# Columns of x on SyncE's queue, a pair's last quarter ahead of the down sums, gate results at the key latents' place

## The reference

```python
z = u @ w_in[l]                      # u = rms_norm(h, g_mix[l])
c_q, c_kv, k_r, rq, rk, rv, rg, gates = jnp.split(z, cuts, axis=-1)
q = (rms_norm(c_q, g_q_lat[l]) @ w_uq[l]).reshape(B, S, MLA_HEADS, MLA_NOPE + MLA_ROPE)
kv = (rms_norm(c_kv, g_kv_lat[l]) @ w_ukv[l]).reshape(B, S, MLA_HEADS, MLA_NOPE + MLA_V)
o_a = causal_block_attention(q_full, k_full, v_a, ...)
y_a = o_a.reshape(B, S, MLA_WIDTH) @ w_proj_mla[l]
y_r = (jax.nn.silu(rg) * y_ret) @ w_proj_ret[l]
g_a, g_r = jnp.split(jax.nn.sigmoid(gates + b_gate[l]), 2, axis=-1)
h = h + (g_a * y_a + g_r * y_r) @ w_out[l]
```

## Time and profile before

| | |
|---|---|
| median of 3 runs | 1813.04 us (1811.16 to 1816.38) |
| the profiled execution | 1813.21 us |
| its span, first to last instruction | 1811.4 us |
| TensorE busy | 1745.7 us, 96% |
| VectorE busy | 1175.9 us, 65% |
| GpSimd busy | 958.8 us, 53% |
| ScalarE busy | 734.4 us, 41% |
| mean granted TensorE clock | 0.991 |

### The profile page before, as it was taken

One profiled execution on the slowest core, in us unless ns is written; L12 is line 12 of the kernel. 1 busy time (PEld: TensorE's weight loads), 2 busy tenths in 40 slices (PEclk: granted clock), 3 DMA queues, 4 the chain that ended last, 5 costly groups with the idle time before them and its releaser, 6 DMA issues. The chain is left out here.

```text
span 1811.4 us, 25039 instructions
## 1 busy us (share of the span) xinstructions
PE 1745.7 (96%) x8527; PEld 1454.3 (80%) x8527; DVE 1175.9 (65%) x1637; ACT 734.4 (41%) x1307; POOL 958.8 (53%) x564
## 2 busy tenths in 40 slices
PE   7999999999989899979999999999999999999998
PEld 7888888888777777768878888778888888878887
DVE  5655663555757777864245554878777777889842
ACT  7422223333315666611133331644454444444432
POOL 6743333335564777634432322487777777665540
PEclk9999999999999999999999999999999999999999
DMA  6611111326763888481221224243333433494322
GB/s 267 208 47 35 41 40 47 117 88 219 272 227 137 324 315 305 172 279 70 93 81 47 70 82 162 71 133 118 124 134 106 139 122 109 163 334 160 122 76 93
DMA packets 119634, 260.30 MB, mean 144 GB/s; under 512 B 7936, under 2 KB 58752, under 8 KB 115072
## 3 DMA queue, kind: packets, MB, share of 16 engines
q1 hardware_dynamic: 84656, 180.03, 29.7%
q10 hardware_dynamic: 34896, 79.18, 11.9%
HBM read 184.73 MB, written 73.92 MB: 143 GB/s over the span
## 5 line engine op out<-in xcount | busy, mean ns | idle before, releaser
L724 POOL TENSOR_SCALAR wh<-raw 128x1024 fp32r<-128x1024 f32 x59 | 167.7, 2842 | 414.0 <-PE ps L841 380.4
L1636 ACT ACTIVATE wh<-raw 128x512 fp32r<-128x512 f32 (+1 forms) x200 | 128.0, 651 | 133.7 <-PE ps L1517 58.1
L773 POOL TENSOR_TENSOR wl<-raw,wh 128x512 fp32r<-128x512 f32 x88 | 136.7, 1564 | 72.1 <-ACT wh L1636 70.9
L841 PE MATMUL ps<-uh,wh 128*128 128x512 f32 x368 | 147.3, 400 | 6.4 <-DVE cql L2491 5.7
L760 POOL TENSOR_TENSOR over_rings<-over_rings 128x512 f32<-128x512 f32 x92 | 118.2, 1286 | 52.8 <-DMA over_rings<-in_slabs 47.3
L726 POOL TENSOR_TENSOR wl<-raw,wh 128x1024 fp32r<-128x1024 f32 x59 | 143.1, 2425 | 4.9
L847 PE MATMUL ps<-uh,wl 128*128 128x512 f32 x368 | 144.7, 393 | 0.0
L846 PE MATMUL ps<-ul,wh 128*128 128x512 f32 x368 | 144.5, 393 | 0.0
L816 POOL TENSOR_TENSOR wl<-raw,wh 128x512 fp32r<-128x512 f32 x63 | 94.4, 1507 | 74.2 <-ACT wh L1636 74.1
L2491 DVE SCALAR_TENSOR_TENSOR ya<-zA,sm,ya 128x512 f32<-128x512 f32 x88 | 109.6, 1245 | 31.9 <-ACT ya L2315 24.8
L1587 PE MATMUL ps<-mvh_,wh 128*128 128x512 f32 x252 | 98.3, 390 | 1.2 <-DVE mvl_ L2488 1.0
(11 more groups left out here) (529 smaller groups left out, 5292.8 us busy)
## 6 DMA issues: line engine op xcount, KB each, us to landing
raw<-in_slabs SPq DMA_DIRECT2D x106, 512.0 KB, 3.6
over_rings<-in_slabs SPq DMA_DIRECT2D x22, 1024.0 KB, 7.1
s_s<-over_rings SPq DMA_DIRECT2D x22, 1024.0 KB, 4.9
ssm<-s_s SPq DMA_DIRECT2D x22, 512.0 KB, 4.5
raw<-s_s SPq DMA_DIRECT2D x22, 512.0 KB, 3.7
s_f<-yb ACTq DMA_DIRECT2D x22, 512.0 KB, 5.3
raw<-s_d SPq DMA_DIRECT2D x36, 256.0 KB, 2.5
raw<-in_slabs SPq DMA_DIRECT2D x27, 256.0 KB, 4.8
```

What stands on the lines that cost most here:

```text
L724: pool.tensor_scalar(wh[:, j, :], raw[:, j % RAWS, :], 1.0, None, ALU.mult).then_inc(S["w_hi"], 1)
L773: pool.tensor_tensor(wl[:, v // 2, half(v % 2)], src, wh[:, v // 2, half(v % 2)].bitcast(f32), ALU.subtract).then_inc(S["v_ready"], 1)
L841: l = pe.matmul(o, lh, rh, start=start, stop=False, skip_group_check=onto)
L1636: return act.activation(o, i, ACT.Copy, **kw)
```

## The change

It has three parts.

1. The columns of x are issued by SyncE. `vr` is laid out head by head, so that head m has the 4 KB of column m, and a column's load waits for `m_pv` of its head. Columns 0 and 1 are issued in the ring's loop (n = 13 and 17), 2 to 4 behind the second mix slab, 5 behind the fourth, 6 and 7 behind the third and the fourth slab of w_out.
2. In the gate pairs, VectorE makes c21 of a pair at the end of that pair's round and ahead of A1 and the down sums, and no longer at the start of the next round. In the last round c21 and the product B0 come ahead of the down sums.
3. gzA and gzB move to the place of ckh and ckl, and gu2, gu4, gx1, gyB1, gyA and gyB0 to that of cqh and cql. The wait for the last gate stores moves on ScalarE from ahead of the first latents to ahead of ckh, behind the first query rows. VectorE waits for its own last product (`gp_mul`) in place of the stores.

```diff
+COLUMN_AT = (13, 17)
+COLUMN_BEHIND = {1: (2, 3, 4), 3: (5,), 6: (6,), 7: (7,)}
...
-        gu2, gu4, gzA, gzB, gyA, gyB1, gyB0, gx1, dsum_gates = place(64, [
-            ("gu2", [P, H2], 0), ("gu4", [P, H2], 0), ("gzA", [P, T], 0), ("gzB", [P, T], 0), ("gyA", [P, T], 0),
-            ("gyB1", [P, H2], 0), ("gyB0", [P, 2, H2], 0), ("gx1", [P, H2], 0), ("dsum_gates", [P, 2, T], 0)])
+        gu2, gu4, gx1, gyB1, gyA, gyB0, gzA, gzB, dsum_gates = place(64, [
+            ("gu2", [P, H2], 0), ("gu4", [P, H2], 0), ("gx1", [P, H2], 0), ("gyB1", [P, H2], 0), ("gyA", [P, T], 0),
+            ("gyB0", [P, 2, H2], 0), ("gzA", [P, T], 0), ("gzB", [P, T], 0), ("dsum_gates", [P, 2, T], 0)])
...
-        vr, qrow, qr1, qr2 = place(0, [("vr", [P, NT, MH, 2, DV], 1),
+        vr, qrow, qr1, qr2 = place(0, [("vr", [P, MH, NT, 2, DV], 1),
...
+            def residual_in(m):
+
+                sp.wait_ge(S["m_pv"], 2 * m + 2)
+                sp.dma_start(hT[:, m, :].rearrange("p (t n) -> p t n", t=NT),
+                             x[:, m * P:(m + 1) * P].rearrange("(t p) n -> p t n", p=P)).then_inc(
+                    S["x_ld0" if m < CH else "xc_ld"], 16)
+
+            def mix_slab(s):
+                sp.wait_ge(S["w_ready"], s - RAWS + 1)
+                sp.dma_start(raw[:, s % RAWS, :], slabs[s - 2 * KB]).then_inc(S[f"ld{s % RAWS}"], 16)
...
+                if n in COLUMN_AT:
+                    residual_in(COLUMN_AT.index(n))
...
-            slab_loads(SLAB0["mix"], SLAB0["xo"], 2 * KB)
+            for s in range(SLAB0["mix"], SLAB0["out"] + SLOTS):
+                mix_slab(s)
+                for m in COLUMN_BEHIND.get(s - SLAB0["mix"], ()):
+                    residual_in(m)
+            slab_loads(SLAB0["out"] + SLOTS, SLAB0["xo"], 2 * KB)
...
-            for name in ("zA0", "zA1", "zB0", "zB1"):
-                act.wait_ge(*gz_store(name, GP))
             for j in range(4):
...
                 if t == 0:
+                    for name in ("zA0", "zA1", "zB0", "zB1"):
+                        act.wait_ge(*gz_store(name, GP))
                     for b in range(2):
                         act.wait_ge(S["l_c"], b + 1)
                         copy(ckh[:, half(b)], lz[:, QB, half(b)]).then_inc(S["l_hi"], 1)
...
-            for m in range(CH):
-                residual_in(m)
-
-
             for m in range(KB):
...
-                if m < CH:
-                    residual_in(CH + m)
...
-                if i:
-                    quarter(i - 1, "c21")
                 quarter(i, "u2")
...
                 quarter(i, "c12")
+                if more:
+                    quarter(i, "c21")
                 if i >= 2:
                     gate_times(i, "A1")
+                if not more:
+                    quarter(i, "c21")
+                    gate_times(i, "B0")
                 if i >= 1:
                     down_sums(i - 1)
-            quarter(GP - 1, "c21")
-            gate_times(GP - 1, "B0")
-
-
-            for name in ("zA0", "zA1", "zB0", "zB1"):
-                dve.wait_ge(*gz_store(name, GP))
+
+
+            dve.wait_ge(S["gp_mul"], gm_at(GP - 1, "B0"))
```

More of the change, by code:

```diff
@@ L1280, in m_pv @@
                     qs = slice(max(0, c - CH * b) * P, H2)
-                    l = pe.matmul(ps[:, 1, qs], vr[:, c, h, :, :].rearrange("p a n -> p (a n)"), p[:, c, qs],
+                    l = pe.matmul(ps[:, 1, qs], vr[:, h, c, :, :].rearrange("p a n -> p (a n)"), p[:, c, qs],
                                   start=k == 0, stop=k == len(each) - 1, skip_group_check=True)
@@ L2007, in value_rows_hi @@
                 act.wait_ge(S["v_done"], MB + t + 1)
-                copy(vr[:, t, :, 0, :], ps[:, 2 + t % 4, :].rearrange("p (h n) -> p h n", h=MH)).then_inc(S["v_evh"], 1)
+                copy(vr[:, :, t, 0, :], ps[:, 2 + t % 4, :].rearrange("p (h n) -> p h n", h=MH)).then_inc(S["v_evh"], 1)
             for t in range(NT):
@@ L2917, in value_rows_lo @@
                 dve.wait_ge(S["v_evh"], t + 1)
-                lo(vr[:, t, :, 1, :], ps[:, 2 + t % 4, :].rearrange("p (h n) -> p h n", h=MH),
-                   vr[:, t, :, 0, :]).then_inc(S["v_lo"], 1)
+                lo(vr[:, :, t, 1, :], ps[:, 2 + t % 4, :].rearrange("p (h n) -> p h n", h=MH),
+                   vr[:, :, t, 0, :]).then_inc(S["v_lo"], 1)
             R = slice(NOPE, QK)
```

## The result

| | before | changed |
|---|---|---|
| median, runs taken side by side | 1812.57 us (4 runs) | 1793.24 us (1791.27 to 1796.82, 4 runs) |
| ratio, 95% interval | | 0.9892 [0.9870, 0.9914] |
| profiled execution: span | 1811.4 us | 1795.0 us |
| mean granted clock of it | 0.991 | 0.991 |

The kernel is faster by 19.3 us; forecast were 22.8.

What follows compares the result with a forecast made beforehand. TensorE's queue was taken to bound the kernel; 12.3 (mix) + 1.6 (gu) + 8.9 (latents) = 22.8 us off the profiled 1813.2 gave 1790.4 us, range 1787.0 to 1798.8.

Steps and rivals of the forecast that it cites:

- Mix wait: TensorE before the output product: 10.1 us idle plus half clock behind it, held by ScalarE's column issues; gain 12.3 us.
- Waits on gu: TensorE's two waits on ScalarE's copy of a gate pair's first product go with c21 sooner; gain 1.6 us.
- Latent wait: TensorE's wait on cql, low half of the query latents: 5.9 us plus 3.0 of half clock, gain 8.9 us.
- Last pair: Last gate pair before the latents: cql written near 508.5, at 512.8 if two products are stretched; no stall taken.
- Rival 1: Down sums between B0 and cql are stretched and make the latents late: 1795.2 us, chance 0.15.
- Columns in the ring: Columns 0 and 1 in SyncE's up-sums ring before the mix slabs: 3 us each against 8.2 cover, costing nothing.
- rivals 3 and 4: Ring ends late: 3, 6.4 us a column, 1798.0 us (0.08); 4, issue and landing stop it, 1829.4 us (0.02).
- Rival 2: Mix hangs on tiles in a full DMA system, only four issues' time is won: 1798.5 us, chance 0.08.
- Attention: Stretch from the query rows' first product to the first product on oth: forecast gain 0.
- The rest: Stretch from the first product on ach to the end, code not touched: forecast gain 0.

Runs made afterwards that it cites:

- columns_alone: Kernel before with part 1 alone (columns of x issued by SyncE, vr head by head): 1801.25 us, ratio 0.9942.
- two_on_scalar: Changed kernel with columns 2 and 3 of x issued by ScalarE again, ahead of its first mih: 1800.62 us, ratio 0.9925.
- order_alone: Kernel before with part 2 alone (VectorE's new order) and vr head by head, waits on the gate stores kept: 1806.13 us, ratio 0.9968.
- order_columns: Changed kernel with part 3 undone (gate tiles and waits on their last stores as before): 1792.02 us, ratio 0.9873.
- sums_first: Changed kernel with the last round's order as before, four down sums ahead of c21 and B0: 1794.49 us, ratio 0.9887.
- columns_late: Changed kernel with all columns issued by SyncE during the mix, behind the sixth, seventh and eighth mix slabs: 1796.17 us, ratio 0.9893.

## Why the prediction was right, and where it was off

- **Mix wait, 12.3 us: right.** 11.7 to 12.3 us in the three profiles (mix and the stretch behind it). columns_alone has it alone, two_on_scalar brings it back. Wrong was a picture beside it: VectorE was to catch up early and then follow TensorE. It had work until the end and cost 0.4 us, because its products are stretched by GpSimd's splits (mil 2.90 us in place of 0.69) about once in 11 us, which I had counted only around the latents. From the first mil to the last a half-block took it 2.38 us, not the 1.93 of the prediction.
- **Waits on gu, 1.6 us: right.** Both are gone.
- **Latent wait, 8.9 us: the total about right, its ground wrong.** I booked it to the moved waits. The profile of order_alone shows that the new order alone removes it, and order_columns that the new places add nothing that can be measured. The step that failed was to take the store's wait as fixed: its landing moves with the last product, and I had computed that the product comes some 9 us sooner. The size was off as well: with gu the step earned 9.4, 7.8 and 10.2 us of the 10.5. In two of the three profiles a new stretch at half clock behind the 32 light products took 1.7 and 3.4 us back; and before's own wait varies (5.7 and 3.1 us in the two profiles that have it).
- **Last pair, no stall: right, with less room than it sounds.** Forecast was cql between 508.5 and 512.8, measured 511.02. The longest stretch fell on a sum (2.86 us). Rival 1 was 1.2 us away. Where its order was undone (sums_first) a wait of 1.6 us stood.
- **Columns in the ring, 3 us each under a cover of 8.2: too dear.** With two, four or none the ring ended alike within its spread of 2 us. The first mix slab was split by 739.84 and first used at 748.01, again 8.2 us ahead, 1.2 of which is the longer wait on prow. Nothing of what rivals 3 and 4 forecast came.
- **Rival 2, only the issuing is saved:** its 5.9 us of wait did not come; of its mechanism columns_late shows 1.1 us. Its rule is that another issuing engine saves only the sequencer's time, usually small beside the DMA's (the Trainium skill, DMA: Bandwidth & Descriptors, section "Issuing engines are not separate DMA queues"). The first half held here. The second did not: two issues held ScalarE for 9.3 us in two_on_scalar, in front of work.
- **Attention, nothing: 0.4 to 1.4 us lost.** The step that failed was to let the attention move as one block. GpSimd's first split falls elsewhere against VectorE's otl. In the nine profiles whose third otl took 2.0 us or more the attention took 199.8 to 200.9 us, in the five others 198.7 to 199.5. Why the split moved is in part open: with no column in the ring wl began 0.9 to 2.1 us ahead of that otl, with columns 0.1 to 0.6 in eight of nine profiles (2.1 in sums_first), so the columns may have a share in it. The Trainium skill, SBUF — State Buffer, section "Who interferes with whom", says that of two such instructions the second waits for the first; here the otl that began within wl ended 0.54 to 0.56 us behind wl's end in all 14 profiles. Beside wh, the other half of the split, the rule holds only in part (last section). I had used the rule for the latents and not for this place.
- **The rest, nothing:** 3.3, -0.2 and 2.2 us against one profile of before. Code that no kernel touched took 889.4 to 895.1 us, and its time at half clock accounts for these differences to 1.2 us. That the change has no part in it is not shown: the three profiles without part 1 have 3.4 to 6.8 us at half clock there, the eleven with it 3.4 to 13.7.

## What to carry to other kernels

A wait for a DMA is gone as soon as the DMA is issued early enough: when a change moves both the issue and the wait, price each alone, or one of them may be superfluous. A DMA issue can hold its engine for microseconds: one of these columns took 0.96 us in the ring and 4.7 us on average behind twelve gate tiles. So such loads belong on an engine with nothing urgent behind them, and early. No run here shows whether the number of pieces or the tiles ahead make them dear. When all work in front of a stage moves, look again at every pair of VectorE and GpSimd instructions near a wait: their overlap changes, and 2 us more for one of them cost TensorE 1.2 us here.

## What the runs showed that I had not expected

- Which of GpSimd's instructions holds VectorE: above all the one of the split that has two inputs (wl<-raw,wh). Every VectorE instruction of 128x512 with two inputs in SBUF that began within a 128x1024 wl ended 0.54 to 0.56 us behind it, 294 of 294 in the 14 profiles (starts within 0.02 us of wl's left out): otl, the sum at 507.08 (wl there until 509.39), the product at 502.88 (wl until 503.73). During wh<-raw only the start of it holds them:

```profile
786.88 1.57 DVE L3036 TENSOR_TENSOR sac<-sac,mrc 128x512 f32<-128x512 f32 x1
788.37 0.68 DVE L2496 TENSOR_TENSOR mil<-sac,mih 128x512 fp32r<-128x512 f32 x1
```

```profile
786.87 2.78 POOL L742 TENSOR_SCALAR wh<-raw 128x1024 fp32r<-128x1024 f32 x1 [5.04 <-PE ps L859]
```

  The one that starts together with wh takes 1.57 us, the next, still beside wh, its usual 0.68. It need not start together with it. In the kernel before:

```profile
742.77 1.19 DVE L2488 TENSOR_TENSOR otl<-oT,oth 128x512 fp32r<-128x512 f32 x1
```

```profile
742.38 2.77 POOL L724 TENSOR_SCALAR wh<-raw 128x1024 fp32r<-128x1024 f32 x1 [8.91 <-DMA raw<-in_slabs]
```

  This otl began 0.39 us behind wh and took 1.19 us; it ended 1.19 us ahead of wh's end. So did all 257 such instructions that began in the first 0.9 us of a wh (1.19 or 1.20 us ahead). The 232 that began 1.45 to 2.3 us behind its start took at most 0.70.
- The clock fell behind the 32 light products in most profiles without TensorE having stopped, and in some of the same kernel it did not. Why is open. Such stretches cost 1.7 or 3.4 us each, here and elsewhere in the program, and go with part of the spread of this kernel's times: over the changed kernel's 14 runs the granted clock goes from 0.991 (1796.5 and 1796.8 us) to 0.996 (1790.7 us), but the shortest run, 1789.2 us, has 0.993.
